# A mixture-of-experts encoder layer on one core: x1 loads moved, logits of the last tile in a bank of their own, g2 products dealt out anew

## The reference

```
mod = SiLU(c) W_ada + b_ada -> sh1, sc1, g1, sh2, sc2, g2        # six rows of 1024 for each sequence
h  = x*(1+sc1)+sh1 ;  mix = token_mixer(h)                       # ends in a 1024 x 1024 product
x1 = LN(ALPHA*x + g1*mix)
h2 = x1*(1+sc2)+sh2
logits = h2 W_router + b            # 4 groups, 32 experts: best group, 2 best experts in it
y  = sum over the 2 picks of w * (SiLU(h2 Wg_e) * (h2 Wu_e)) Wd_e
out = LN(ALPHA*x1 + g2*y)
```

## Time and profile before

| | us |
|---|---|
| median of 3 runs (lowest, highest) | 1294.38 (1293.54, 1296.82) |
| the profiled execution, its own time | 1293.76 |
| its span, first to last instruction | 1292.0 |
| TensorE busy | 1238.0 (96%) |
| VectorE busy | 954.9 (74%) |
| ScalarE busy | 643.8 (50%) |
| mean DMA rate over the span | 255 GB/s |

### The profile page before, as it was taken

One profiled execution on the slowest core, in us unless ns is written; L12 is line 12 of the kernel. 1 busy time (PEld: TensorE's weight loads), 2 busy tenths in 40 slices (PEclk: granted clock), 3 DMA queues, 4 the chain that ended last, 5 costly groups with the idle time before them and its releaser, 6 DMA issues.

```text
span 1292.0 us, 23415 instructions
## 1 busy us (share of the span) xinstructions
PE 1238.0 (96%) x6513; PEld 1021.3 (79%) x6514; DVE 954.9 (74%) x1197; ACT 643.8 (50%) x669; POOL 205.6 (16%) x244
## 2 busy tenths in 40 slices
PE   7999999999999989899999999999999999999693
PEld 6888999998888865688888888888888888888451
DVE  5767556456999987965797556745888998886497
ACT  5553221122222243654777555645777788776421
POOL 0011110000101002311122111111212122122032
PEclk9999999999999999899999999999999999999897
DMA  9944221025323576866899666955999999998983
GB/s 313 279 132 132 72 93 33 18 93 188 145 98 114 194 299 262 341 246 243 332 397 405 258 238 232 347 224 217 383 401 402 395 400 388 400 396 297 356 295 128
DMA packets 121646, 329.09 MB, mean 255 GB/s; under 512 B 12040, under 2 KB 43904, under 8 KB 121604
## 3 DMA queue, kind: packets, MB, share of 16 engines
q1 hardware_dynamic: 107412, 288.08, 59.6%
q0 software_dynamic: 12320, 34.15, 7.4%
q10 hardware_dynamic: 1872, 6.29, 1.2%
HBM read 296.97 MB, written 39.42 MB: 260 GB/s over the span
## 4 chain that ended last, share of the span: by engine, by line
PE 73%; DVE 15%; issue 4%; DMA 3%; ACT 2%; POOL 2%; SPq 2%; ACTq 0%; DVEq 0%; POOLq 0%
PE bank L1688 18%; PE bank L1690 18%; PE bank L1689 18%; PE bank L1701 3%; PE bank L1703 3%; PE bank L1702 3%; PE bank L1995 3%; POOL rstd L745 1%; PE bank L2019 1%; DVE h L1403 1%; ACT w_mid L985 1%; DVE fin L1647 1%; DVE fin L1662 1%; DVE gated L1643 1%; DMA sh2b<-mod_rows 1%
## 5 line engine op out<-in xcount | busy, mean ns | idle before, releaser
L1539 DVE TENSOR_TENSOR gu_l<-gu_raw,gu_h (+1 forms) x128 | 287.4, 2288 | 43.7 <-ACT gu_h L1011 41.7
L1688 PE MATMUL bank<-gu_h,xT_h 128*128 (+1 forms) x624 | 247.9, 397 | 2.0 <-DVE xT_l L1558 1.4
L1011 ACT ACTIVATE gu_h<-gu_raw (+1 forms) x128 | 238.7, 1926 | 13.4 <-issue 12.6
L1690 PE MATMUL bank<-gu_h,xT_l 128*128 (+1 forms) x624 | 244.2, 391 | 0.0
L1689 PE MATMUL bank<-gu_l,xT_h 128*128 (+1 forms) x624 | 243.7, 391 | 0.0
L1543 DVE TENSOR_TENSOR dn_l<-dn_raw,dn_h (+1 forms) x64 | 143.6, 2286 | 5.9 <-ACT dn_h L1015 5.9
L1688 PEld LDWEIGHTS bank<-gu_h,xT_h 128*128 128x128 f32 x624 | 117.8, 189 | 25.8 <-issue 2.3
L1690 PEld LDWEIGHTS bank<-gu_h,xT_l 128*128 128x128 f32 x624 | 117.6, 188 | 25.0
L1689 PEld LDWEIGHTS bank<-gu_l,xT_h 128*128 128x128 f32 x624 | 118.0, 189 | 23.3
L1688 PE MATMUL bank<-dn_h,aT_h 128*128 (+1 forms) x312 | 125.0, 401 | 2.5 <-DVE aT_l L1553 2.5
L1690 PE MATMUL bank<-dn_h,aT_l 128*128 (+1 forms) x312 | 121.8, 390 | 0.0
(11 more groups left out here) (308 smaller groups left out, 2178.4 us busy)
## 6 DMA issues: line engine op xcount, KB each, us to landing
gu_raw<-in_w_gate_up SPq DMA_DIRECT2D x128, 1024.0 KB, 7.8
dn_raw<-in_w_down SPq DMA_DIRECT2D x64, 1024.0 KB, 7.6
y<-y_rows SPq DMA_DIRECT2D x24, 512.0 KB, 5.9
ada_raw<-in_w_ada SPq DMA_DIRECT2D x20, 512.0 KB, 7.3
ada_raw<-in_w_ada SPq DMA_DIRECT2D x10, 1024.0 KB, 5.4
win_raw<-in_w_in SPq DMA_DIRECT2D x8, 768.0 KB, 8.9
h_rows<-h SPq DMA_DIRECT2D x12, 512.0 KB, 2.6
fin<-x_rows SPq DMA_DIRECT2D x12, 512.0 KB, 9.5
```

What stands on the lines that cost most here:

```text
L1011: nc.scalar.activation(gu_slot(gu_h, e, c), gu_slot(gu_raw, e, c), ACT.Copy).then_inc(S["gu_split_h"], 1)
L1539: nv.tensor_tensor(gu_slot(gu_l, e, c), gu_slot(gu_raw, e, c), gu_slot(gu_h, e, c).bitcast(F32), ALU.subtract).then_inc(S["gu_split_l"], 1)
L1688: mm(out, lh, rh, start=start, stop=False)
L1690: return mm(out, ll, rh, start=False, stop=stop)
```

## The change

1. SP loads x1 of tiles 0 to 5 where it loaded all twelve. The other six are issued in pairs behind the y rows of tiles 3, 4 and 5. The semaphores now hold two groups of six (96).
2. Tile 11's logits go to bank 5 instead of 6. `route(11)` then no longer waits for `logits_out(10)`, and `logits_out(10)` moves ahead of `x1_out(11)`.
3. The 16 g2 products are dealt out anew: one before `rank(4)`, three before the transposes of tile 11, one before `route(11)`, three before `rank(5)`, then 2, 3 and 3. The two `warm` calls of the mix's end (4 and 2 products) are gone.
4. ScalarE's wait for `g2_added` stands in block 0 behind the three `high_gu`, before `silu(0)`.

```diff
-        x1_loaded = [sem(f"x1_loaded{g}") for g in range(NT // 4)]
+        x1_loaded = [sem(f"x1_loaded{g}") for g in range(2)]
...
-            for t in range(NT):
-                sp.dma_start(fin[t][:], x1_d[bass.ds(t * P, P), :]).then_inc(x1_loaded[t // 4], 16)
+
+            def load_x1(t):
+                sp.dma_start(fin[t][:], x1_d[bass.ds(t * P, P), :]).then_inc(x1_loaded[t // 6], 16)
+
+            for t in range(6):
+                load_x1(t)
...
                 sp.dma_start(y1[s][:], y_d[bass.ds(T + t * P, P), :]).then_inc(y_loaded[s], 16)
+                if 3 <= t < 6:
+                    load_x1(2 * t)
+                    load_x1(2 * t + 1)
...
             act.wait_ge(S["eid_ready"], 1)
-            act.wait_ge(S["g2_added"], 16)
...
                     for c in range(3):
                         high_gu(e_next, c)
+                if first:
+                    act.wait_ge(S["g2_added"], 16)
                 silu(i)
...
-                nv.tensor_tensor(logits[:, t, :], ps[6][:, 0:NG + NE], router_b[:], ALU.add).then_inc(S["logit_read"], 1)
+                nv.tensor_tensor(logits[:, t, :], ps[5 if t == NT - 1 else 6][:, 0:NG + NE], router_b[:], ALU.add).then_inc(S["logit_read"], 1)
...
                 if t == NT - 1:
                     picks(4)
+                    logits_out(t - 1)
                 x1_out(t)
...
-                if t >= 2:
+                if 2 <= t < NT - 1:
                     logits_out(t - 1)
                     if t % 2 == 0:
                         select(t // 2 - 1)
-                    elif t < NT - 1:
+                    else:
...
-                dve.wait_ge(x1_loaded[t // 4], 64)
+                dve.wait_ge(x1_loaded[t // 6], 96)
...
                 pe.wait_ge(S["h2T_copied"], t + 1)
-                if t >= 1:
+                if 1 <= t < NT - 1:
                     pe.wait_ge(S["logit_read"], t)
                 for k in range(KD):
-                    last = mm(ps[6][:, 0:NG + NE], h2T[:, k, :], router_w[:, k, :], start=k == 0, stop=k == KD - 1)
+                    last = mm(ps[5 if t == NT - 1 else 6][:, 0:NG + NE], h2T[:, k, :], router_w[:, k, :], start=k == 0, stop=k == KD - 1)
...
+            g2_part(0, 1)
             rank(4)
             route(NT - 2)
-            g2_part(0, 1)
-            warm(1, 4)
+            g2_part(1, 4)
             h2_transposes(NT - 1)
-            g2_part(1, 2)
+            g2_part(4, 5)
             route(NT - 1)
             pick(4)
-            g2_part(2, 6)
-            warm(1, 2)
+            g2_part(5, 8)
             rank(5)
...
-            g2_part(6, 8)
+            g2_part(8, 10)
             pick(5)
...
-            g2_part(8, 12)
+            g2_part(10, 13)
...
-            g2_part(12, 16)
+            g2_part(13, 16)
```

## The result

The changed kernel takes 1285.05 us (median of 4 runs, 1283.7 to 1285.74) where the kernel before took 1294.95 on the same chip (4 runs): ratio 0.9922, 95% interval 0.991 to 0.9935. That is 9.9 us faster; 14.7 were forecast. The profiled execution has a span of 1282.7 us where it was 1292.0: 9.3 less.

What follows compares the result with a forecast made beforehand. The chain of waits was 73% TensorE and 15% VectorE, so gains lay where TensorE waits or in VectorE's final stage. Front 7.8 and tail 6.9 sum to 14.7 us: median 1279.7, range 1276 to 1286.5, own range 1276 to 1283.5.

Steps and rivals of the forecast that it cites:

- The edits of the mix's end: End of the mixer: tile 11's logits 2.1 us earlier, rank(5)'s result 3.3, table of experts 4.2; bounds 0.5 to 4.8.
- The moved wait, up to gate_up(1): Block 0: ScalarE splits without waiting for g2_added; act_a comes at 513.2, gate_up(1) at 515.9, 7.0 us earlier.
- Rival 2: Front held: fillers at the lower clock, table no earlier, gather sets gate_up(1), only 3.0 us left; 1284.5, chance 0.15.
- TensorE, which has no wait of size from there to the last block, carries this to the end: From gate_up(1) through the expert blocks: the whole front gain of 7.8 us, bounds 3.0 to 9.2, reaches the end.
- The 0.8 credited for the clock of gate_up(1): Block 1's start: TensorE's half clock had cost 2.2 us; 0.8 was taken back, bounds 0 and 2.2.
- Rival 3: Expert loop: weight loads set its pace, so the front's gain is only waited away later; 1287.5 us, chance 0.04.
- x1 behind y: Tail: six x1 loads leave the queue ahead; scatter lands 3.1 us earlier, final sums start 5.6 earlier.
- rival 1: Tail: the scatter isn't freed and lands at 1207.4, leaving a tail gain of 2.5 us; 1284.1, chance 0.15.
- The clock of the final sums: First final tile: the half clock after idling had lost 2.8 us; 1.3 was taken back, bounds 0 and 2.8.
- rival 5: Final stage: slower, as tile 6 waits for the late x1 loads; 1299 us if they land at 1265; chance 0.03.
- no change: Whole kernel: nothing of the change is on the path, so the time stays 1294.4 us; chance 0.03.
- the case in which both clock losses vanish: TensorE's low-clock losses at gate_up(1), 2.2 us, and the final sums, 2.8, both go; said to lie below 1276.

Runs made afterwards that it cites:

- weights_in_gaps: Changed kernel, moved wait included, with VectorE's scatter table and picks' weights moved to where VectorE waits; 1279.82 us, ratio 0.9879.
- x1_only: Kernel before with only the x1 loads of tiles 6 to 11 put behind the y rows; 1290.99 us, ratio 0.9967.
- fillers_block1: Changed kernel with TensorE's block 1 written out ahead of its loop and eight small products before and eight after the activation's transposes; 1283.06 us, ratio 0.9908.
- list_only: Kernel before with only tile 11's logits in bank 5 and the g2 products dealt out anew; 1289.18 us, ratio 0.9954.
- changed_again: The changed kernel itself, timed once more beside the kernel before in a later group; 1285.74 us, ratio 0.9921.
- wait_only: Kernel before with only ScalarE's wait for g2_added moved behind the three splits; 1297.61 us, ratio 1.0014.
- front_only: Changed kernel with all twelve x1 loads back ahead of y; 1291.27 us, ratio 0.9963 to the kernel before.
- peel_only: Changed kernel with TensorE's block 1 written out ahead of its loop and no added products; 1283.98 us, ratio 0.9914.
- no_wait_move: Changed kernel with ScalarE's wait for g2_added back ahead of block 0, all else as changed; 1283.11 us, ratio 0.9907.

## Why the prediction was right in part

**The edits of the mix's end: right.** Tile 11's logits were forecast at 480.65 and came at 480.26; rank(5)'s result at 486.4 and 485.93; the table at 493.7 and 493.25; gate_up(0) at 501.2 and 501.00. The three g2 products ahead of the transposes of tile 11 (2.74 us from 472.43) did not delay them: they began at 475.62, where it was 475.89.

**The moved wait, up to gate_up(1): right.** act_a(0) was forecast at 513.2 and came at 512.91, gate_up(1) at 515.9 and 515.86. Rival 2's mechanism is refuted by these.

**"TensorE, which has no wait of size from there to the last block, carries this to the end": this step failed.** It is right from block 2 on: the column "to last block" is 636.5 to 636.8 in all fourteen kernels. It is wrong for block 1. In the kernel before, VectorE worked with one gap, of 1.17 us, from act_a(0) at 519.98 to act_a(1):

```profile
540.48 0.68 DVE L1549 TENSOR_TENSOR act_a<-bank,act_s 128x512 f32<-128x512 f32 x1
```

20.5 us, and TensorE took up its transposes 1.2 after it ended, with no wait. Two engines were thus nearly level, and I had followed only the one. Counted from tile 10's copy, the gain goes like this:

- act_a(0): 7.3 us.
- act_a(1): 4.9. VectorE now waits 0.61 and 1.62 us, the second for a split that itself waits for its weights to land.
- The transposes of act_a(1): 6.0. The 1.2 us by which TensorE was the later one before have gone, and it waits 2.48 us for VectorE.
- gate_up(2): 4.0. The idle time ahead of it is 2.66 us instead of 0.67. About 0.5 of it is VectorE's subtraction of x, which ends after the transposes; the runs don't show what the other 2.2 are.
- Block 2's transposes of x: 1.9. At the lower clock that block's gate products take 13.1 us instead of 11.0.

weights_in_gaps shows that VectorE's way is the cause of the first loss and of the wait for it, by shortening it: there 8.8 of the front arrive (85.91 less 77.12), where 7.8 were forecast. That the idle time and the clock recover with it is seen in its trace; that they must is not shown. The other executions put the changed kernel's own front gain between 1.9 and 4.3, by the spread of 1.2 in that column.

**The 0.8 credited for the clock of gate_up(1) was no gain.** The clock there did stay at 1.00. But before, TensorE ended block 1 only 1.2 us behind VectorE, so no more than about 1.1 of the 2.2 us lost there had been on the path; and now VectorE set the block's end, so that what TensorE won became part of its wait of 2.48.

**Rival 3, that the loop gives the front back,** has the outcome right for that part and the mechanism mostly wrong: the weights' landing costs 0.78 us once, ahead of block 1, and from block 2 on nothing is given back. Its chance of 0.04 was too low for the reason above.

**x1 behind y: right.** From the last transposes to the sums 5.6 us less were forecast; 5.1 and 5.2 came in the profiles of the changed kernel and 5.2 in x1_only; kernels with twelve loads ahead have 23.5 to 24.0 there, those with six 18.4 to 19.3. The scatter took 4.4 to 5.5 us in the ten kernels with six (5.2 in the changed one) and 7.6 to 8.4 in the four with twelve, so rival 1 is refuted. By the Trainium skill (DMA: Bandwidth & Descriptors, Queues, rings and completion order) each DMA engine takes turns between queues with work. That a scatter on another queue would then keep its 7.7 us was my reading of it, and it doesn't fit this trace: a shorter backlog on SP's queue freed 2.5 to 3. The runs don't show whether turns or the shared engines' bandwidth do that.

**The clock of the final sums: right in kind, low in size.** 1.3 of the 2.8 us were credited; 2.5 to 2.6 came in both profiles and in most kernels with six loads ahead, but only 0.9 to 1.0 in x1_only and fillers_block1. That is no more than list_only has (75.86) with the old tail, so of these two it isn't shown that they gained anything here. Before, TensorE idled 8.4 us ahead of the sums, in x1_only and fillers_block1 3.2 and 3.8, and in the others 1.7 at most.

**Tile 6** waits for nothing; rival 5 is refuted, and so is no change.

Front 7.8 against 1.9, tail 6.9 against 7.7, and 0.2 of the start and 0.1 of the loop lost by chance: 14.7 against 9.3 in the profile, 9.9 in the medians.

**Where it was luck.** The median of 1285.05 lies beyond the forecast's own range, which ended at 1283.5. It lies in the wider one only through the room left for rivals 1 and 2, whose 1284.1 and 1284.5 it nearly meets while the mechanisms of both are refuted. The tail made good 0.8 of what the front lost.

Two figures of the working are off: 7.3 less 4.37 is 2.9 and not 2.8, and the case in which both clock losses vanish (9.2 and 8.4, so 1276.8) lies inside the range and not below it. Neither changes the account.

## What to carry to other kernels

Before crediting a gain on one engine to the end, walk the other engines' chains through the next step of the pipeline too: where one has no idle time there, it carries only what its own start gains, and what the first engine brings beyond that turns into idle time, and here into a lower clock as well. Look for one-time work on that chain that can go into its waits: 3.6 us of tables moved into gaps gave about 5 us of the median. In a tail, count the loads queued ahead of the one that is waited for: those not needed yet could stand behind it here at no cost. And small products that go nowhere are not free where the engine has no wait: two groups of 1.95 us cost 2.1 of the path here.

## What the runs showed of the hardware

- TensorE's clock went to 0.50 (1.2 GHz) in block 2 after an idle time of 2.48 us, four transposes and 2.66 more (changed), after 2.53 and 2.15 (changed_again), 2.49 and 2.26 (wait_only), and even 1.32 and 1.73 (front_only). It stayed at 1.00 after 1.35 and 1.43 (peel_only), none and 1.43 (no_wait_move), none and 1.41 (weights_in_gaps). front_only and peel_only are nearly alike there and came out on different sides. A fall there cost 1.6 us (changed_again, wait_only) to 2.6 (front_only), over gate products that take 11.0 at the full clock.
- A fall whose loss another engine covers cost nothing here. The gate products of block 1 took 12.6 us at a mean clock of 0.86 in front_only and peel_only and 11.0 at 1.00 in the changed kernel, and TensorE then waited 1.32, 1.35 and 2.48 us for VectorE.
- The idle time "issue" of TensorE ahead of gate_up(2) was 0.56, 0.67 and 0.96 us in list_only, before and x1_only, 1.4 in no_wait_move, peel_only and weights_in_gaps, and 1.7 to 2.7 in the others with the moved wait. Part of it is VectorE's subtraction of x, which gate_up(2) needs: from its end to gate_up(2) it is 0.9 to 1.4 us in seven kernels, but 1.8 in wait_only and 2.1 and 2.2 in the two profiles of the changed kernel. The runs don't show the cause of the rest.
- The start of the whole kernel varied: with the same code, tile 10's copy was at 468.3 to 471.3, and the first 50 us had a mean clock of 0.97 in the changed kernel and 0.90 in no_wait_move_fill. A single profile can't settle 3 us between kernels; the same event later on, counted from a common one, can settle about 1.
